# Block inversion in a macaron hybrid layer: four transposed copies made by VectorE instead of TensorE

## The reference, cut to what matters

```python
m = jnp.where(strict, jnp.einsum("bnhid,bnhjd->bnhij", k_beta, k) * decay, 0.0)
tri = m + jnp.eye(CHUNK, dtype=m.dtype)          # CHUNK = 64
u = lax.linalg.triangular_solve(tri, v_beta, left_side=True, lower=True, unit_diagonal=True)
w = lax.linalg.triangular_solve(tri, k_beta * jnp.exp(gc)[..., None], left_side=True, lower=True, unit_diagonal=True)
...
def step(S, inp):                                # RWKV-7, one token at a time
    sa = jnp.einsum("bhij,bhj->bhi", S, a_t)
    S = S * w_t[:, :, None, :] + sa[..., None] * b_t[:, :, None, :] + v_t[..., None] * k_t[:, :, None, :]
    return S, jnp.einsum("bhij,bhj->bhi", S, r_t)
```

## Time and profile before

| | value |
|---|---|
| median of 3 runs | 2993.47 us |
| profiled execution, its own time | 3000.16 us |
| its span | 2998.4 us |
| TensorE busy | 2909.7 us, 97% |
| VectorE busy | 1532.0 us, 51% |
| ScalarE busy | 1232.5 us, 41% |
| mean granted clock | 0.97 of full |

### The profile page before, as it was taken

One profiled execution on the slowest core, in us unless ns is written; L12 is line 12 of the kernel. 1 busy time (PEld: TensorE's weight loads), 2 busy tenths in 40 slices (PEclk: granted clock), 3 DMA queues, 4 the chain that ended last, 5 costly groups with the idle time before them and its releaser, 6 DMA issues.

```text
span 2998.4 us, 40095 instructions
## 1 busy us (share of the span) xinstructions
PE 2909.7 (97%) x16440; PEld 2374.9 (79%) x16440; DVE 1532.0 (51%) x1605; ACT 1232.5 (41%) x1386; POOL 34.1 (1%) x63
## 2 busy tenths in 40 slices
PE   8999999999999899999999899999899999999998
PEld 6888888888877677776787788888688888888886
DVE  5555555544564545522631666565465555555444
ACT  5444444444552526222521554333244444444443
POOL 0000000000000000000000000000000000000000
PEclk9999999999999999987996999999999999999999
DMA  6666666555653434323430755555256666666554
GB/s 209 188 188 191 187 187 190 191 193 177 180 155 106 148 114 147 100 71 93 148 90 32 251 205 189 184 189 175 70 190 191 189 188 189 190 188 203 194 193 147
DMA packets 259569, 495.45 MB, mean 165 GB/s; under 512 B 17769, under 2 KB 28236, under 8 KB 259052
## 3 DMA queue, kind: packets, MB, share of 16 engines
q1 hardware_dynamic: 250528, 470.21, 50.7%
q0 software_dynamic: 3856, 14.29, 1.5%
q10 hardware_dynamic: 5052, 9.03, 0.9%
HBM read 480.89 MB, written 12.58 MB: 165 GB/s over the span
## 4 chain that ended last, share of the span: by engine, by line
PE 50%; DVE 2%; ACT 0%; issue 0%; DMA 0%; DVEq 0%; ACTq 0%
PE pp L319 15%; PE pp L320 15%; PE pp L321 15%; PE pa L379 1%; PE pa L770 1%; PE pb L1709 1%; PE pb L770 0%; PE pp L1733 0%; PE pb L1338 0%; PE pa L1317 0%; PE pb L1337 0%; PE pa L1318 0%; PE pa L1303 0%; DMA gs<-proj 0%; PE pa L1323 0%
## 5 line engine op out<-in xcount | busy, mean ns | idle before, releaser
L280 DVE TENSOR_TENSOR wlo<-raw,whi 128x1024 fp32r<-128x1024 f32 (+1 forms) x888 | 1078.7, 1220 | 1067.3 <-ACT whi L275 1066.6
L275 ACT ACTIVATE whi<-raw 128x1024 fp32r<-128x1024 f32 (+1 forms) x888 | 932.5, 1055 | 1195.4 <-PE pp L321 1166.5
L319 PE MATMUL pp<-whi,xhi 128*128 128x512 f32 x2336 | 943.0, 404 | 10.1 <-DVE wlo L280 9.1
L320 PE MATMUL pp<-whi,xlo 128*128 128x512 f32 x2336 | 922.3, 395 | 0.0
L321 PE MATMUL pp<-wlo,xhi 128*128 128x512 f32 x2336 | 921.5, 394 | 0.0
L319 PEld LDWEIGHTS pp<-whi,xhi 128*128 128x128 f32 x2336 | 446.7, 191 | 112.8 <-DVE wlo L280 11.7
L321 PEld LDWEIGHTS pp<-wlo,xhi 128*128 128x128 f32 x2336 | 447.1, 191 | 94.6
L320 PEld LDWEIGHTS pp<-whi,xlo 128*128 128x128 f32 x2336 | 447.7, 192 | 86.2
L319 PE MATMUL pp<-whi,hhi 128*128 128x512 f32 x704 | 274.7, 390 | 0.0
L321 PE MATMUL pp<-wlo,hhi 128*128 128x512 f32 x704 | 274.3, 390 | 0.0
L320 PE MATMUL pp<-whi,hlo 128*128 128x512 f32 x704 | 274.2, 390 | 0.0
(11 more groups left out here) (380 smaller groups left out, 2172.0 us busy)
## 6 DMA issues: line engine op xcount, KB each, us to landing
raw<-in_ffn_w_gate SPq DMA_DIRECT2D x176, 512.0 KB, 3.7
raw<-in_ffn_w_up SPq DMA_DIRECT2D x176, 512.0 KB, 3.7
raw<-in_ffn_w_down SPq DMA_DIRECT2D x176, 512.0 KB, 3.6
raw<-in_w_in SPq DMA_DIRECT2D x144, 512.0 KB, 3.7
raw<-in_w_lift SPq DMA_DIRECT2D x32, 512.0 KB, 5.4
raw<-in_w_out SPq DMA_DIRECT2D x32, 512.0 KB, 4.3
raw<-in_w_mk SPq DMA_DIRECT2D x32, 512.0 KB, 3.9
raw<-in_w_mv SPq DMA_DIRECT2D x32, 512.0 KB, 4.2
```

What stands on the lines that cost most here:

```text
L275: nc.scalar.activation(whi[:, s, :, 0:width], raw[:, s, :, 0:width], ACT.Copy).then_inc(whi_ready, 1)
L280: nc.vector.tensor_tensor(wlo[:, s, :, 0:width], raw[:, s, :, 0:width], whi[:, s, :, 0:width].bitcast(F32), ALU.subtract).then_inc(wlo_rea ...
L319: nc.tensor.matmul(out, a_hi[:, k0 + k, tok], w_hi, start=first, stop=False)
L320: nc.tensor.matmul(out, a_lo[:, k0 + k, tok], w_hi, start=False, stop=False)
```

## The change

The transposed copies come from VectorE's 32x32 transpose. `a` and its powers are zero outside the diagonal blocks of 16, so a transpose of every 32x32 block by itself is the transpose of the whole. Four are made so: `b` from `a`, `d` from `c`, `b` from `a` (fourth power), `d` from `e`. Eight steps are left, eleven products of 16 matrices, twelve counted VectorE operations instead of nine, four ScalarE copies instead of seven. The table loses two tiles per inversion (one for the second, which had a zero). The total of the table is then 270, not 281 cut at 272.

```diff
-    "inv0": [1, 1, 1, 1, 1, 1, 1, 1, 1, 1],
+    "inv0": [1, 1, 1, 1, 1, 1, 1, 1],
...
-    "inv1": [1, 1, 1, 1, 1, 1, 1, 0, 1, 1],
+    "inv1": [1, 1, 1, 1, 1, 1, 1, 1],
...
-        INV_MM, INV_DVE, INV_ACT = 10, 9, 7
+        INV_MM, INV_DVE, INV_ACT = 8, 12, 4
...
-            pe.wait_ge(sem("inv_in"), v + 1)
-            blocks(units[0], a, eye).then_inc(mm_done, 1)
+            pe.wait_ge(by_dve, dv + 2)
+            blocks(units[1], b, a).then_inc(mm_done, 1)
             mark(1)
-            pe.wait_ge(by_act, ac + 1)
-            blocks(units[1], b, a)
-            blocks(units[2], a, b).then_inc(mm_done, 1)
+            pe.wait_ge(by_dve, dv + 4)
+            blocks(units[0], d, c)
+            blocks(units[1], d, e).then_inc(mm_done, 1)
             mark(2)
-            pe.wait_ge(by_dve, dv + 2)
-            pe.wait_ge(by_act, ac + 2)
-            blocks(units[0], d, c)
-            blocks(units[3], c, d)
-            blocks(units[1], d, e).then_inc(mm_done, 1)
-            mark(3)
-            pe.wait_ge(by_dve, dv + 4)
-            pe.wait_ge(by_act, ac + 3)
+            pe.wait_ge(by_dve, dv + 6)
+            pe.wait_ge(by_act, ac + 1)
             blocks(units[2], a, b)
             blocks(units[0], b, e).then_inc(mm_done, 1)
-            mark(4)
-            pe.wait_ge(by_dve, dv + 5)
-            pe.wait_ge(by_act, ac + 4)
+            mark(3)
+            pe.wait_ge(by_dve, dv + 7)
+            pe.wait_ge(by_act, ac + 2)
             blocks(units[1], c, e).then_inc(mm_done, 1)
-            mark(5)
-            pe.wait_ge(by_dve, dv + 6)
-            blocks(units[2], e, eye).then_inc(mm_done, 1)
-            mark(6)
-            pe.wait_ge(by_act, ac + 5)
+            mark(4)
+            pe.wait_ge(by_dve, dv + 9)
             blocks(units[0], d, f)
             blocks(units[3], f, d).then_inc(mm_done, 1)
...
+            def turn_blocks(n, dst, src):
+                dve.wait_ge(sem("inv_dve"), INV_DVE * v + n)
+                v_.transpose(dst[:, :, :].rearrange("p u c -> p (u c)"), src[:, :, :].rearrange("p u c -> p (u c)")).then_inc(sem("inv_dve"), 1)
+
             v_.tensor_tensor(e[:, :, :], a[:, :, :], over_units(eye), ALU.add).then_inc(sem("inv_dve"), 1)
+            turn_blocks(1, b, a)
             bg_dve(dve, f"inv{v}.1")
+            step(1, lambda: v_.tensor_copy(c[:, :, :], units[1]))
+            turn_blocks(3, d, c)
+            step(2, lambda: v_.tensor_tensor(e[:, :, :], e[:, :, :], units[1], ALU.add))
+            dve.wait_ge(sem("inv_act"), INV_ACT * v + 1)
+            turn_blocks(5, b, a)
             bg_dve(dve, f"inv{v}.3")
+            step(3, lambda: v_.tensor_tensor(e[:, :, :], e[:, :, :], units[0], ALU.add))
             bg_dve(dve, f"inv{v}.4")
+            dve.wait_ge(sem("inv_dve"), INV_DVE * v + 7)
+            step(4, lambda: v_.tensor_tensor(e[:, :, :], e[:, :, :], units[1], ALU.add))
+            turn_blocks(8, d, e)
+            bg_dve(dve, f"inv{v}.5")
+            step(5, lambda: v_.tensor_copy(a[:, :, :], units[0]))
```

More of the change, by code:

```diff
@@ L79, in inversion @@
     def inversion(v):
-        section(f"inv{v}", [f"inv{v}.{k + 1}" for k in range(10)])
+        section(f"inv{v}", [f"inv{v}.{k + 1}" for k in range(8)])
     for hf in range(HALVES):
@@ L107 @@
     "rw0.mats0": [2],
-    "inv2": [1, 1, 1, 1, 1, 1, 1, 1, 1, 1],
+    "inv2": [1, 1, 1, 1, 1, 1, 1, 1],
     "rw0.mats1": [2],
-    "inv3": [1, 1, 1, 1, 1, 1, 1, 1, 1, 1],
+    "inv3": [1, 1, 1, 1, 1, 1, 1, 1],
     "rw0.chunks": [1, 1, 1, 1, 1, 1, 1, 1, 1, 1, 0, 1],
@@ L114 @@
     "rw1.mats0": [2],
-    "inv4": [1, 1, 1, 1, 1, 1, 1, 1, 1, 1],
+    "inv4": [1, 1, 1, 1, 1, 1, 1, 1],
     "rw1.mats1": [2],
-    "inv5": [1, 1, 1, 1, 1, 1, 1, 1, 1, 1],
+    "inv5": [1, 1, 1, 1, 1, 1, 1, 1],
     "rw1.chunks": [1, 1, 1, 1, 1, 1, 1, 1, 1, 1, 1, 1],
@@ L774, in mark @@
                 bg_pe(pe, f"inv{v}.{k}")
-            pe.wait_ge(sem("inv_in"), v + 1)
-            blocks(units[0], a, eye).then_inc(mm_done, 1)
+            pe.wait_ge(by_dve, dv + 2)
+            blocks(units[1], b, a).then_inc(mm_done, 1)
             mark(1)
-            pe.wait_ge(by_act, ac + 1)
-            blocks(units[1], b, a)
-            blocks(units[2], a, b).then_inc(mm_done, 1)
-            mark(2)
-            pe.wait_ge(by_dve, dv + 2)
-            pe.wait_ge(by_act, ac + 2)
-            blocks(units[0], d, c)
@@ L786, in invert_pe @@
-            blocks(units[3], c, d)
-            blocks(units[1], d, e).then_inc(mm_done, 1)
-            mark(3)
-            pe.wait_ge(by_dve, dv + 4)
-            pe.wait_ge(by_act, ac + 3)
+            pe.wait_ge(by_dve, dv + 4)
+            blocks(units[0], d, c)
+            blocks(units[1], d, e).then_inc(mm_done, 1)
+            mark(2)
+            pe.wait_ge(by_dve, dv + 6)
+            pe.wait_ge(by_act, ac + 1)
             blocks(units[2], a, b)
             blocks(units[0], b, e).then_inc(mm_done, 1)
+            mark(3)
@@ L793, in invert_pe @@
+            pe.wait_ge(by_dve, dv + 7)
+            pe.wait_ge(by_act, ac + 2)
+            blocks(units[1], c, e).then_inc(mm_done, 1)
             mark(4)
-            pe.wait_ge(by_dve, dv + 5)
+            pe.wait_ge(by_dve, dv + 9)
+            blocks(units[0], d, f)
+            blocks(units[3], f, d).then_inc(mm_done, 1)
+            mark(5)
+            pe.wait_ge(by_dve, dv + 10)
+            pe.wait_ge(by_act, ac + 3)
+            blocks(units[2], a, b).then_inc(mm_done, 1)
+            mark(6)
@@ L795, in invert_pe @@
             pe.wait_ge(by_act, ac + 4)
             blocks(units[1], c, e).then_inc(mm_done, 1)
-            mark(5)
-            pe.wait_ge(by_dve, dv + 6)
-            blocks(units[2], e, eye).then_inc(mm_done, 1)
-            mark(6)
-            pe.wait_ge(by_act, ac + 5)
-            blocks(units[0], d, f)
-            blocks(units[3], f, d).then_inc(mm_done, 1)
             mark(7)
-            pe.wait_ge(by_dve, dv + 7)
-            pe.wait_ge(by_act, ac + 6)
-            blocks(units[2], a, b).then_inc(mm_done, 1)
+            pe.wait_ge(by_dve, dv + 11)
@@ L808, in invert_pe @@
+            blocks(units[0], b, d).then_inc(mm_done, 1)
             mark(8)
[L809 to L814, removed]
         def invert_act(act, v, buf, spool):
             a, b, c, d, e, f = buf
-            for step, dst, u in ((1, b, 0), (2, d, 2), (3, b, 3), (4, c, 2), (6, d, 2), (7, b, 3), (8, c, 2)):
+            bg_act(act, f"inv{v}.1", spool)
@@ L819, in invert_act @@
+            for step, dst, u in ((2, a, 0), (3, c, 2), (5, b, 3), (6, c, 2)):
                 act.wait_ge(sem("inv_mm"), INV_MM * v + step)
                 copy(act, dst[:, :, :], units[u]).then_inc(sem("inv_act"), 1)
-                bg_act(act, f"inv{v}.{step if step not in (4, 8) else step + 1}", spool)
-            bg_act(act, f"inv{v}.10", spool)
+                bg_act(act, f"inv{v}.{step if step != 3 else 4}", spool)
+            bg_act(act, f"inv{v}.8", spool)
         def invert_dve(dve, v, buf, out):
@@ L831, in invert_dve @@
             v_ = nc.vector
+            def turn_blocks(n, dst, src):
+                dve.wait_ge(sem("inv_dve"), INV_DVE * v + n)
+                v_.transpose(dst[:, :, :].rearrange("p u c -> p (u c)"), src[:, :, :].rearrange("p u c -> p (u c)")).then_inc(sem("inv_dve"), 1)
             v_.tensor_tensor(e[:, :, :], a[:, :, :], over_units(eye), ALU.add).then_inc(sem("inv_dve"), 1)
+            turn_blocks(1, b, a)
             bg_dve(dve, f"inv{v}.1")
[L834 to L837, removed]
+            step(1, lambda: v_.tensor_copy(c[:, :, :], units[1]))
[3 more added lines that the diff above has]
+            turn_blocks(5, b, a)
             bg_dve(dve, f"inv{v}.3")
-            step(4, lambda: v_.tensor_tensor(e[:, :, :], e[:, :, :], units[0], ALU.add))
+            step(3, lambda: v_.tensor_tensor(e[:, :, :], e[:, :, :], units[0], ALU.add))
             bg_dve(dve, f"inv{v}.4")
-            step(5, lambda: v_.tensor_tensor(e[:, :, :], e[:, :, :], units[1], ALU.add))
+            dve.wait_ge(sem("inv_dve"), INV_DVE * v + 7)
[3 more added lines that the diff above has]
+            step(5, lambda: v_.tensor_copy(a[:, :, :], units[0]))
             bg_dve(dve, f"inv{v}.6")
-            step(7, lambda: v_.tensor_copy(a[:, :, :], units[0]))
+            step(7, lambda: v_.tensor_tensor(d[:, :, :], e[:, :, :], units[1], ALU.add))
+            bg_dve(dve, f"inv{v}.7")
+            step(8, lambda: v_.tensor_tensor(out, d[:, :, :], units[0], ALU.add))
             bg_dve(dve, f"inv{v}.8")
[L845 to L848, removed]
             dve.wait_ge(sem("inv_dve"), INV_DVE * (v + 1))
```

## The result

The changed kernel takes 3008.75 us (median of 7 executions, 2998.68 to 3012.3) against 2993.47: a ratio of 1.0042 with an interval of 1.0025 to 1.006. By the ratio it is slower by 12.6 us, by the medians by 15.3, where 8.5 less were forecast. Its profiled execution took 3012.3 us, span 3010.4; that of before 3000.16, span 2998.4. One execution of the kernel of experiment 4 took 4737.04 us, in a slow state with a granted clock of 0.55 in all, and is left out of the figures given for it.

What follows compares the result with a forecast made beforehand. TensorE, busy 97% of the span, was taken as the bound: -42.4 + 12.9 + 0.8 + 6.6 + 13.5 = -8.6 us, against the median of 2993.47 a forecast of 2985 us, range 2975 to 2999.

Steps and rivals of the forecast that it cites:

- The bound: Whole kernel: TensorE is busy 97% of the span, so what is taken off it counts, unless it then waits.
- 24.15 worked out: Each inversion after the change: 24.15 us of TensorE's work against 31.35; gain 42.4 us over six if nothing waits.
- The transpose: One VectorE transpose of 512 floats per partition was priced at 0.70 us, with ends 0.43 and 1.22.
- the rival with 1.22: Transposes take 1.22 us, delaying first products and steps 2, 3, 5: +12.5 us, 2997.4; chance 0.14.
- Added wait 1: Before each inversion's first product, for `e = a + I` and its transpose: 12.9 us over six.
- The tail: Last rw1 chunk to second lift product: 41.4 us instead of 28.6; 13.5 us given back including 0.7 for the clock.
- eleven moved tiles: Background tiles moved from the inversions to the end: 15.1 us of work, 13.5 us charged there.
- Added wait 2: Inside inversions, add or copy then transpose at steps 2, 3, 5, rounding ahead at step 5: 0.8 us over six.
- The clock: Granted clock falls behind four of the new waits, 1.65 us each: 6.6 us; ends 0 and 8.3.
- the clock didn't hold: Rival: clock holds through the new waits, all 6.6 us stay, 2978.3 us; chance 0.22.
- the end took what was forecast for it: Rival: background's end at low clock, 11 moved tiles cost 28 us instead of 13.5, 2999; chance 0.10.
- slower at all: Outcome slower above 3002.5 us: 0.11, from slow transpose 0.05, expensive end 0.04 and the remainder 0.02.

Runs made afterwards that it cites:

- experiment 4: Changed kernel with the first transposed copy by TensorE again, table's sums kept, ScalarE going on to later marks behind its copies: 2972.5 us (0.9924).
- experiment 3: Changed kernel with ScalarE going on to a later mark behind each of its copies, so its roundings come sooner: 3001.17 us (1.0021).
- experiment 7: Kernel of experiment 3 with one background tile more in the second inversion (nine instead of eight): 2985.1 us (0.9966).
- experiment 1: Kernel before the change with one background tile more, in the second inversion; no transpose in it: 3012.0 us (1.0057).
- experiment 6: Kernel before the change with two background tiles more (a whole slot) in the second inversion: 2994.09 us (0.9995).
- experiment 8: Changed kernel with VectorE's e = a + I and first transpose put ahead of the roundings of `mats`: 2998.43 us (1.0012).
- experiment 10: Changed kernel with the queue edits of experiment 3 and experiment 8 and the table's sums of tiles kept: 2973.22 us (0.9928).
- 5: Same kernel as experiment 4, run a second time for a profile: 2977.52 us (0.993).

## Why the prediction was wrong

**Right.** The bound and the reading of the earlier trace rows: the inversion is TensorE's own work, and with the other waits and the clock out of the way it takes 24.35 us against 24.15 worked out (experiments 3 and 7). The transpose: 0.70 taken, 0.711 measured, so the rival with 1.22 is out. The Trainium skill ("Vector Engine (DVE) Microarchitecture Reference", section 3.8) says that the transpose sustains one element per cycle per lane; the trace agrees as far as the rows beside it can tell, 512 floats in 0.711 us where the ordinary operations take 0.68. Its rule that a semaphore between two VectorE operations costs nothing ("VectorE: DVE Perf Modes", "The DRAIN you can't avoid") is not borne out here either: from the add to the transpose that waits for it are 0.72 us (1497.11 to 1497.83), from the mask to the rounding that doesn't wait for it 0.60 (1495.38 to 1495.98). Added wait 1: forecast 2.47, 2.07 and 0.9, measured 2.48 three times, 2.08 and 0.94; in the third inversion the same wait lies in a stage that is 4.8 us longer. The tail: 41.4 us from the last chunk to the second lift product forecast, 41.42 measured (1645.56 to 1686.98), and by the links of the working: 13.14 to L1345 in both. Behind it 0.7 were forecast for the clock and 1.5 measured.

**The step that failed most was left out.** The sum has a term for the eleven moved tiles at their new place only, and puts what taking them out does to the stages between at nothing, without a reason. Taking them out changed which half of a slot each later tile is. The table gives 122 tiles up to rw0 before, 119 after, 123 and 124 in experiments 1 and 6, and 120 in experiment 7: the odd ones lose. Experiments 1 and 6 show the price without the change (17 us for one tile, nothing for two), experiment 7 within it (16 us back by one tile). Between the profiles of 3 and 7, 11.2 us of this can be placed: 3.0 in rw0 ahead of its masks, 1.4 between the transposition of rw0's result and rw1's first own product, 3.2 from there to rw1's masks, 1.3 in the mask stage ahead of the third inversion, and 2.3 (0.96, 0.70 and 0.69) in waits at the end of the second, fourth and sixth. The rest isn't traced. In the changed kernel that mask stage lost 2.3, at clock 0.77 behind the wait of 3.44, and the three ends 0.97, 0.69 and 0.69. Of its 9.6 us ahead of the rw masks the first two parts, 1.9 and 1.3, go with the half slot in all runs (75.5 us and more against 73.9 and less; 12.2 against 10.8 to 10.9). Of the third, 6.4, about half stands in the even kernels of experiments 6 and 7 too (80.1 us against 76.8 before and 83.2 after), so that half is not the half slot's, and nothing here shows whose it is. The 3.5 of the chunk loops are within what their clock alone does.

**Added wait 2 was mis-sized: 0.8 forecast, 3.8 measured,** 1.91 and 1.92 in the first inversion (with the three waits of the half slot 6.2 in all six). The working looked for a rounding ahead of the product of step 5 in the inversions with an even running total. In the odd one the waits stand ahead of the product of step 4, which the working doesn't mention, and that of step 6, which it has under "nothing". ScalarE does the rounding there only behind its own copy, 0.12 + 0.60 + 1.05 us less a small overlap after the product, and VectorE's half comes in front of the add (step 3) or copy (step 5) that TensorE needs. Experiment 3 takes both out by moving ScalarE's roundings to earlier marks.

**The clock was mis-sized: 6.6 forecast, about 12 measured** (19.2 us above six times 24.15, less 6.2 of waits and 6 x 0.2), and this counts the inversions alone. The size of one fall was nearly right (1.5 against 1.65, experiment 7). Their number was not: all six inversions were touched, the first through wait 2, and the third and fourth by 2.7 us each. The experiment that shortened the waits (8) got the clock back in four, but the two that didn't (3 and 7) in three each, so the number of falls can't be had from the lengths of the waits.

Of the rivals the clock didn't hold, the transposes weren't slow, and the end took what was forecast for it, not 28 us. That it could be slower at all was given 0.11, all of it for prices of things in sight; no case was held for an effect of the shift itself.

## What to carry to other kernels

Where background work is cut finer than the buffers that feed it, moving one piece moves every later cut. Compare the running total modulo the buffer at each stage, not only the number of pieces, and try the change with the total made even. Take a copy off the critical engine only where something covers its latency: with three of the four transposes, and ScalarE's roundings in time, the kernel is 0.7% faster than before. The fourth, between whose input and reader nothing is left in rw, cost more there than the product that it replaced (up to 0.9 us, experiment 10 beside 5), and less in gdn, where tiles cover it. When both halves of a rounding sit in two queues, look at which copy each half stands behind.

## What the runs showed of the hardware that was not expected

Waits of the same length left the clock at full or not: of those of 2.69 to 2.77 us in experiment 7 two did and two didn't, with the same products behind them. Nor does the clock stay at full where TensorE never waits: a rw chunk of the same instructions takes, among others, 16.1, 18.4, 20.3 or 24.9 us at a granted clock of 1.00, 0.85, 0.75 or 0.57, and in one of 24.9 in the kernel before TensorE is busy from end to end:

```profile
1321.90:1346.80 24.90, 24.90 (x147) 18.31 (x146) 2.11 (x4) 2.83 (x4) 0.00 (x0) 0.57 0.15 43
```

Which of these clocks a chunk gets changes from kernel to kernel, with nothing changed in the chunk itself. That is as large as the effect of a typical edit here, so a single profile can't rank two versions that differ by 5 us.
